# The down product of a SwiGLU block as seven block products (Strassen) in place of eight, interleaved with the next slab's first gate and up units

## The reference

```python
SEQ, D_MODEL, D_FF = 512, 2048, 5632
def reference(x, norm_mix_g, norm_ffn_g, nsa_w_in, ..., ffn_w_gate, ffn_w_up, ffn_w_down):
    h = rms_norm(x, norm_mix_g[i])
    x = x + nsa_mixer(h, ...)
    h = rms_norm(x, norm_ffn_g[i])
    x = x + (silu(h @ wg) * (h @ wu)) @ wd
```

## Time and profile before

| | us |
|---|---|
| median of 3 runs | 2411.09 (2411.08 to 2411.6) |
| profiled execution, first to last instruction (span) | 2406.7 |
| the median less that span | 4.4 |
| last piece of unbroken PE work in the chain that ended last | 967.95 to 2399.60 |
| end of the last add into x2 | 2402.11 |

### The profile page before, as it was taken

The page is one execution under the profiler, slowest core; times in us unless marked ns, Lnnn a source line. Parts: engine busy times, 40 slices in busy tenths (PEclk is TensorE's granted clock), DMA queues, the critical chain, the costliest instruction groups (busy, mean ns, idle before and its releaser), DMA issues.

```text
span 2406.7 us, 32223 instructions
## 1 busy us (share of the span) xinstructions
PE 2359.4 (98%) x12347; PEld 2021.5 (84%) x12347; DVE 1082.1 (45%) x1852; ACT 698.1 (29%) x1081; POOL 38.6 (2%) x44
## 2 busy tenths in 40 slices
PE   7999999999999999999999999999999999999998
PEld 6898888888889899888888888888888888888887
DVE  5333566665665556433334334343433333333433
ACT  4332344443452334322212122222222221212221
POOL 1000000000010000000000000000000000000000
PEclk9999999999999999999999999999999999999999
DMA  5333211212113212332333333333333233332333
GB/s 174 114 110 90 69 54 46 71 53 63 53 62 132 71 62 80 95 98 89 105 96 96 96 94 98 96 96 96 96 97 96 94 101 99 95 97 89 102 96 114
DMA packets 212815, 218.62 MB, mean 91 GB/s; under 512 B 12715, under 2 KB 186816, under 8 KB 211440
## 3 DMA queue, kind: packets, MB, share of 16 engines
q1 hardware_dynamic: 211792, 211.86, 28.3%
q0 software_dynamic: 928, 5.44, 0.7%
HBM read 213.05 MB, written 4.19 MB: 90 GB/s over the span
## 4 chain that ended last, share of the span: by engine, by line
PE 95%; DVE 3%; ACT 1%; issue 1%; DMA 0%; POOL 0%; DVEq 0%; SPq 0%; ACTq 0%
PE ps L1057 93%; PE ps L1351 1%; DVE wl L623 0%; DMA x_rows<-in_x_dram 0%; PE ps L1343 0%; DVE x_rows L639 0%; DVE nmax L888 0%; PE ps L1387 0%; DVE ptl L908 0%; ACT ptc L369 0%; DVE pbuf L902 0%; ACT sq L372 0%; DVE x_rows L824 0%; DVE ql L623 0%; DVE hTl L623 0%
## 5 line engine op out<-in xcount | busy, mean ns | idle before, releaser
L623 DVE TENSOR_TENSOR wl<-raw,wh 128x1024 fp32r<-128x1024 f32 x386 | 472.3, 1224 | 754.4 <-ACT wh L369 753.4
L1057 PE MATMUL ps<-hTh,wh 128*128 128x512 f32 (+1 forms) x1968 | 768.5, 391 | 6.7 <-DVE wl L623 3.5
L1057 PE MATMUL ps<-hTh,wl 128*128 128x512 f32 (+1 forms) x1968 | 761.9, 387 | 0.0
L1057 PE MATMUL ps<-hTl,wh 128*128 128x512 f32 (+1 forms) x1968 | 761.1, 387 | 0.0
L369 ACT ACTIVATE wh<-raw 128x1024 fp32r<-128x1024 f32 x386 | 408.7, 1059 | 1016.8 <-PE ps L1057 998.0
L1057 PEld LDWEIGHTS ps<-hTh,wh 128*128 128x128 f32 x1968 | 371.5, 189 | 78.9 <-DVE ql L623 3.6
L1057 PEld LDWEIGHTS ps<-hTh,wl 128*128 128x128 f32 x1968 | 370.7, 188 | 75.1
L1057 PEld LDWEIGHTS ps<-hTl,wh 128*128 128x128 f32 x1968 | 371.1, 189 | 71.6
L1057 PE MATMUL ps<-wh,mTl 128*128 128x512 f32 x704 | 274.3, 390 | 0.0
L1057 PE MATMUL ps<-wh,mTh 128*128 128x512 f32 x704 | 274.3, 390 | 0.0
L1057 PE MATMUL ps<-wl,mTh 128*128 128x512 f32 x704 | 274.3, 390 | 0.0
(11 more groups left out here) (164 smaller groups left out, 1655.0 us busy)
## 6 DMA issues: line engine op xcount, KB each, us to landing
raw<-in_ffn_w_gate_dram SPq DMA_DIRECT2D x176, 256.0 KB, 2.9
raw<-in_ffn_w_up_dram SPq DMA_DIRECT2D x176, 256.0 KB, 2.9
raw<-in_ffn_w_down_dram SPq DMA_DIRECT2D x176, 256.0 KB, 3.2
raw<-in_nsa_w_in_dram SPq DMA_DIRECT2D x164, 256.0 KB, 3.0
raw<-in_nsa_w_out_dram SPq DMA_DIRECT2D x64, 256.0 KB, 3.0
x_rows<-in_x_dram SPq DMA_DIRECT2D x4, 1024.0 KB, 12.2
raw<-in_nsa_cmp_w_dram SPq DMA_DIRECT2D x16, 256.0 KB, 3.0
x_rows<-in_x_dram POOLq DMA_DIRECT2D x4, 1024.0 KB, 7.6
```

The costliest lines, as they stand in the source:

```text
L623: nc.vector.tensor_tensor(dst, src, hi.bitcast(f32), ALU.subtract).then_inc(done, 1)
L1057: return nc.tensor.matmul(out_, a, b, start=start, stop=stop, skip_group_check=True)
```

## The change

The down product of one slab is Y[512 tokens x 2048] += m[512 x 512] W[512 x 2048]. It is now done as two quads of 1024 output columns. In a quad each operand is taken as 2 x 2 blocks, and Strassen's method in Winograd's form needs seven block products where eight stood. A block product (`product`) is 12 matmuls of 128x512 on a weight block of 128x1024 (256 rows of W by 512 columns); it fills two banks. So a slab has 14 down units of 12 matmuls (d0 to d13), and its 16 gate and up units (g0 to g15) stay as they were.

The combinations of weight blocks are made by DVE in `down` and `t3` (`add`: four per quad), and split like any unit. The combinations of m are made by DVE at up units 7 and 15 (four subtractions or adds of 128x256), after which ACT rounds seven operands to `opsh` (three copies) and DVE subtracts to `opsl` (three `lo`). `operands_at` says where that is done: for the second half at g15, for the first half, in a mixed slab, only at d13, since `opsh` and `opsl` of the slab before are in use until then. DVE adds two banks at a time to `x2` after each block product (`down_out`), and PE waits for the add of d(j-2) before d(j).

The down units of a slab no longer follow its own g15. They are mixed with the next slab's first gate and up units: g0 g1 d0 d1, six times (g, d, d), then g8 to g15. The last slab's 14 down units stand alone at the end (`DOWNS`). Slab 0 has only g units (`UPS`); the loop runs over pairs of slabs. The down blocks are loaded into four buffers of their own. At the end there are eight stores of 512 KB.

Core of the diff (ACT's `up_split` and `down_split`, the memory and semaphore declarations and the calls of `slab` on ACT and DVE are left out):

```diff
+G_UNITS, QUAD, DOWN = 16, 7, 14
+TURN = G_UNITS + DOWN
+UPS = [("g", j) for j in range(G_UNITS)]
+MIXED = [("g", 0), ("g", 1), ("d", 0), ("d", 1)] \
+    + [e for r in range(6) for e in (("g", 2 + r), ("d", 2 + 2 * r), ("d", 3 + 2 * r))] + UPS[8:]
+DOWNS = [("d", j) for j in range(DOWN)]
+LEFT = [M0A, M1A, S2, S1, S3, N4, M1B]
...
+        def down_bank(j):
+            return 4 + 2 * ((j // QUAD + j % QUAD) % 2)
+        def operands_at(order, j):
+            if order is DOWNS or order is UPS or j == G_UNITS - 1:
+                return ("g", j)
+            return ("d", DOWN - 1)
...
@@ SP
+                    quad, o = j // QUAD, j % QUAD
+                    if o in (2, 3, 5, 6) and (s < SLABS or quad == 0):
+                        wait(sp, lo_ready, n0 + p + 1, 2 * TURN, i)
+                        down_block({2: 0, 3: 1, 5: 3, 6: 2}[o], s - 1 + quad, i, 1 - quad)
...
@@ ACT
-                    if j in (7, 15):
-                        for c in range(2):
-                            wait(act, m_ready, (j - 7) // 4 + c + 1, 4, s)
-                            copy(mTh[:, (j - 7) // 4 + c, :], ffn_work[:, 2 + c, :]).then_inc(m_hi, 1)
+                    for b in range(2):
+                        if (kind, j) == operands_at(order, 8 * b + 7):
+                            wait(act, m_ready, 2 * s + b + 1, 4, i)
+                            wait(act, units_used, n0 + p + 1, 2 * TURN, i)
+                            copy(opsh[:, b, M0A, :], ffn_work[:, 2, 0:256]).then_inc(m_hi, 1)
+                            copy(opsh[:, b, M1A:M1B + 1, :]..., ffn_work[:, 3, :]).then_inc(m_hi, 1)
+                            wait(act, m_sums, 2 * s + b + 1, 4, i)
+                            copy(opsh[:, b, S1:N4 + 1, :]..., ffn_work[:, 0:2, :]...).then_inc(m_hi, 1)
...
@@ DVE
+            def down_out(n, s, i, j):
...
+                wait(dve, units_used, n + 1, 2 * TURN, i)
+                if after:
+                    wait(dve, y_added, before + after, 2 * DOWN, i)
+                nc.vector.tensor_tensor(at, at, ps[:, down_bank(j):down_bank(j) + 2, :], op).then_inc(y_added, 1)
...
+                        own.done(nc.vector.tensor_tensor(s1, m0b, m1b, ALU.subtract))
+                        nc.vector.tensor_tensor(s3, m0a, m0b, ALU.subtract)
+                        own.settle()
+                        own.done(nc.vector.tensor_tensor(s2, s1, m0a, ALU.subtract))
+                        own.settle()
+                        nc.vector.tensor_tensor(n4, m1a, s2, ALU.add).then_inc(m_sums, 1)
+                    for b in range(2):
+                        if (kind, j) == operands_at(order, 8 * b + 7):
+                            wait(dve, m_hi, 6 * s + 3 * b + 1, 12, i)
+                            lo(opsl[:, b, M0A, :], ffn_work[:, 2, 0:256], opsh[:, b, M0A, :], m_lo)
...
+                    if kind == "d":
+                        down_out(n, s, i, j)
+                    if p + RING < len(ahead):
+                        turn, (what, unit) = ahead[p + RING]
+                        (up_split if what == "g" else down_split)(n + RING, turn, i, unit)
...
@@ PE
+            def product(n, j):
+                o, b = LEFT[j % QUAD], down_bank(j)
+                for tt in range(2):
+                    for kk in range(2):
+                        ts, at = slice(tt * P, (tt + 1) * P), slice(kk * 512, (kk + 1) * 512)
+                        last = mm3(bank(b + tt), (opsh[:, kk, o, ts], opsl[:, kk, o, ts]),
+                                   (wh[:, n % RING, at], wl[:, n % RING, at]), kk == 0 and j % QUAD in (0, 1, 3), kk == 1)
+                last.then_inc(units_used, 1)
...
+                    wait(pe, lo_ready, n + 1, 2 * TURN, i)
+                    if kind == "d":
+                        if j == 0:
+                            wait(pe, m_lo, 6 * s, 12, i)
+                        if j >= 2:
+                            wait(pe, y_added, DOWN * (s - 1) + j - 1, 2 * DOWN, i)
+                        product(n, j)
+                        continue
...
+                    if s and j == 8:
+                        wait(pe, y_added, DOWN * s, 2 * DOWN, i)
+                    hidden_unit(n, j)
```

More of the change, by code:

```diff
@@ L301, in _, with up_unit @@
-            out_v = out[0].rearrange("(t p) d -> p t d", p=P)
[L302 to L306, removed]
+            def up_unit(n, s, i, j):
+                b, q, w = j // 8, j % 8 // 2, (w_gate_v, w_up_v)[j % 2]
+                src = w[q][:, :, bass.ds(i * 1024 + s * 512 + b * 256, 256)]
+                for dst, half in k_halves(n, src, 4):
+                    sp.dma_start(dst, half).then_inc(raw_loaded[n % RAW], 16)
@@ new lines, in _ @@
+            out_v = out[0].rearrange("(t p) d -> p t d", p=P)
+            for quad in range(2):
+                for done, row, half in ((2, 0, 0), (5, 2, 1), (6, 0, 1), (7, 2, 0)):
+                    at = (slice(None), slice(row, row + 2), slice(quad * 1024 + half * 512, quad * 1024 + half * 512 + 512))
+                    sp.wait_ge(y_added, (SLABS - 1) * DOWN + quad * QUAD + done)
+                    sp.dma_start(out_v[at], x2[at]).then_inc(stored, 16)
+            sp.wait_ge(stored, 128)
@@ new lines, in slab @@
+            def slab(order, after, n0, s, i):
+                ahead = [(s, e) for e in order] + [(s + 1, e) for e in after]
+                for p, (kind, j) in enumerate(order):
+                    if s == 0 and j == 1:
+                        hidden_part(3)
+                    if kind == "g" and j in (6, 14):
+                        wait(act, gs_ready, 2 * s + j // 8 + 1, 4, i)
+                        nc.scalar.activation(ffn_work[:, 0:2, :], ffn_work[:, 0:2, :], ACT.Silu).then_inc(silu_done, 1)
+                    for b in range(2):
[3 more added lines that the diff above has]
+                            copy(opsh[:, b, M0A, :], ffn_work[:, 2, 0:256]).then_inc(m_hi, 1)
+                            copy(opsh[:, b, M1A:M1B + 1, :].rearrange("p o c -> p (o c)"), ffn_work[:, 3, :]).then_inc(m_hi, 1)
+                            wait(act, m_sums, 2 * s + b + 1, 4, i)
+                            copy(opsh[:, b, S1:N4 + 1, :].rearrange("p o c -> p (o c)"),
+                                 ffn_work[:, 0:2, :].rearrange("p a c -> p (a c)")).then_inc(m_hi, 1)
+                    if p + RING < len(ahead):
+                        turn, (what, unit) = ahead[p + RING]
+                        (up_split if what == "g" else down_split)(n0 + p + RING, turn, i, unit)
@@ L617, in _ @@
+            slab(UPS, MIXED[:RING], F0, 0, 0)
+            with act.Fori(0, PAIRS) as i:
+                for h in range(2):
+                    slab(MIXED, MIXED[:RING], F0 + G_UNITS + h * TURN, 1 + h, i)
+            slab(MIXED, MIXED[:RING], F0 + G_UNITS + (SLABS - 3) * TURN, SLABS - 2, 0)
+            slab(MIXED, DOWNS[:RING], F0 + G_UNITS + (SLABS - 2) * TURN, SLABS - 1, 0)
+            slab(DOWNS, [], F0 + G_UNITS + (SLABS - 1) * TURN, SLABS, 0)
         @block.vector
@@ L1008, in _, with up_split, add @@
             last.then_inc(r2_diag, 1)
[L1010 to L1013, removed]
+            def up_split(n, s, i, j):
+                wait(dve, hi_ready, n + 1, 2 * TURN, i)
+                lo(wl[:, n % RING, :], raw[:, (F0 + s * G_UNITS + j) % RAW, :], wh[:, n % RING, :], lo_ready)
+            def add(out_, a, b):
+                nc.vector.tensor_tensor(out_, a, b, ALU.add).then_inc(sums_ready, 1)
@@ L1014, in slab @@
+            def slab(order, after, n0, s, i):
+                ahead = [(s, e) for e in order] + [(s + 1, e) for e in after]
+                both = rbc[:, :].rearrange("p (a c) -> p a c", a=1).to_broadcast([P, 2, S])
+                for p, (kind, j) in enumerate(order):
+                    n, b = n0 + p, j // 8
+                    if s == 0 and j == 1:
                         hidden_part(3)
-                    if first and j == 4:
+                    if s == 0 and j == 4:
                         dve.wait_ge(rb_done, 1)
@@ L1037, in slab @@
[L1037 to L1046, removed]
@@ new lines, in slab @@
+                    if kind == "d":
+                        down_out(n, s, i, j)
+                    if p + RING < len(ahead):
+                        turn, (what, unit) = ahead[p + RING]
+                        (up_split if what == "g" else down_split)(n + RING, turn, i, unit)
+            slab(UPS, MIXED[:RING], F0, 0, 0)
+            with dve.Fori(0, PAIRS) as i:
+                own.enter(i, 12)
+                for h in range(2):
+                    slab(MIXED, MIXED[:RING], F0 + G_UNITS + h * TURN, 1 + h, i)
+                own.leave(PAIRS)
@@ L1417, in norm_bcast, with hidden_unit @@
                 last.then_inc(rb_done, 1)
-            def hidden_unit(n, j, per, s):
+            def hidden_unit(n, j):
                 for half in range(2):
                     columns_half(n, j % 8 // 2, half, j // 8 * 4 + j % 2 * 2 + half)
[L1424 to L1428, removed]
+            def product(n, j):
```

(20 more changed lines are left out.)

166 lines of the change are left out of this document (100 added, 66 removed).

## The result

| | before | after |
|---|---|---|
| median, us | 2411.09 (4 runs) | 2439.61 (4 runs, 2437.68 to 2443.74) |
| ratio to before, 95% interval | | 1.0119 [1.0105, 1.0133] |
| span of the profiled execution, us | 2406.7 | 2436.6 |

The change makes the kernel 28.5 us slower. The forecast was 2431, so it is 8.6 us too low; the measured time lies inside the forecast's own range of 2417 to 2446, in its upper quarter.

The account below looks back on a forecast made before the run. PE, busy 98% of the span, was taken as the bound. Terms: -59.8 + 56 + 9.2 - 1.3 - 1.0 + 16.5 = +19.6 us on the 2406.7 span, plus 4.4 to the median: 2431 us; own range 2417 to 2446.

Parts of the forecast that it names:

- The 59.8 us: Down matmuls on PE fall from 192 to 168 a slab, 264 fewer at 0.2267 us each: -59.8 us.
- the third rival: DVE's chain around d13 is shorter than counted: 2360 us if hidden altogether, 2394 with half the wait left; chance 0.06.
- The wait at g8: In each mixed slab PE's g8 waits for DVE's add of d13: 5.6 us, ten times, +56 us.
- The walk: DVE's operations from g7's end on PE to the add of d13 at 10.8 us; g8 starts 5.4 us late.
- The rounds: Mix rounds (g, d, d): DVE needs 11.0 us against PE's 10.88, covered by the ring, costed at nothing.
- The fourth rival: The mix rounds stall too, through DVE's work and late loads: 2 us more a slab, 2451 us; chance 0.08.
- The clock: PE's granted clock falls to half after ten g8 waits and the tail's: 11 x 1.5 = +16.5 us.
- the first rival: The waits are there but the clock stays up: 2414 us, or 2408 to 2422; chance 0.13.
- The second rival: Long cold stretches of 10.2 us follow the waits: 2465 us; chance 0.08.
- The tail: Last slab's down units: d0 waits 6.65 us for m_lo, d7 about 0.6, d8 about 1.9; +9.2 us.
- The end and the start: At the very end, the last store is 512 KB in place of 1024 KB: -1.0 us.

Follow-up runs that it names:

- e5: e4 with DVE's add of d13 also put ahead of the sums of m and the opsl subtractions: 2360.59 us, ratio 0.9794 to the kernel before.
- e1: Kernel after, with DVE's add of d13 issued before the three opsl subtractions: 2418.32 us, ratio 1.003 to the kernel before.
- e2: Kernel after, with g8 waiting only for the add of d12 and g9 for that of d13: 2376.75 us, ratio 0.9859 to the kernel before.
- e4: e2 with the four 128x256 sums of m of the first half made at d13 instead of g7: 2367.41 us, ratio 0.982.
- e3: Kernel after, with 24 matmuls of 128x512, result never read, run on PE ahead of g8's wait: 2419.22 us, ratio 1.0034.
- e6: e5 with d0, d1 and d2 each waiting only for the part of m_lo that they use: 2360.30 us, ratio 0.9784.

## Why the prediction was right, and where it was off

**What bounds.** PE did, and its cadence stayed 0.2267 us with `opsh` as stationary operand: in e5 it shows 3089 matmuls in 700 us, the same spacing. The 59.8 us were there to be had; e5 has them less the tail, and the 2360 us of the third rival, priced for this case, were met at 2360.59.

**The wait at g8.** Mechanism, place and size were right: 5.59 us for 5.6. The last tenths are luck: the walked steps give 5.4, and 5.6 was chosen between that and 6.2. The walk was right step by step: sums done at 4.23 us (measured 1132.44 - 1128.08 = 4.36), add of d12 6.50 (6.64), add of d13 10.8 (10.97). e1 and e2 took pieces out of the chain and the wait fell to 3.4 and 1.1 us, and in e4 to nothing at g8 and 0.3 us at g9. The names in the wait list (L1134 and once `opsl`) and the count of ten at g8 were as forecast.

**The rounds.** Costed at nothing, and they cost nothing: no wait of PE is left between 1000 and 2280 us in e5, with all of DVE's work still in it. The fourth rival is out. Its 11.0 us against 10.88 were also too high: DVE's operations of 1024 columns start 1.13 to 1.14 us apart when nothing holds them, so nine of them take 10.2 us.

**The clock.** The mechanism was right: two of two early waits pointed to it, the first rival (clock stays up) is out, e3 shows 20 us. Its size was too small, and this is the largest error in the sum: 1.5 us a wait taken, 2.2 measured. Two things were missing. The cold stretch was taken as 3.4 us from the earlier trace rows; in the first slab PE works 3.5 us of it, in the nine later ones 4.0 to 4.9 us, by the spacing of the matmuls. And the first matmul after a long wait takes 0.59 us to the next one's start, 0.16 more than the cadence of 0.43 at half clock. At both early waits the clock fell 0.3 and 0.7 us after PE was back and stayed low for 3.4 us. Here it falls while PE stands and stays low for 6.8 us, of which the part after the restart is paid in matmuls; the later the fall, the larger that part. Why a dip lasts 3.4 us in one case and 6.8 in another is open. The second rival's 10.2 us did not appear. One reading of the sum was loose too: of the counts of 8 and 7 in the earlier trace rows, the 8 are from windows that are in part at full clock; the share of 0.45 does come out of the starts in the trace, though, 0.21 us apart against 0.12.

**The tail.** d0's wait was 6.61 (6.65 forecast). The two later ones are 1.83 each, where 0.6 and 1.9 were walked. The missed piece is a transfer: ACT's split for d8 waits 2.81 us in all, the last part for the reload of a down block, which the chain of waits puts at 3.85 us from 2401.21 on. I had costed the loads at nothing for the whole stage; in the tail, without g units between, that cover is gone. DVE's split for d8 waits 1.08 us for ACT there, which is about what the two waits are above the walked sum (3.66 for 2.5). No run moved that load, so its share is read from the chain and not shown by an edit. ACT's row, and the piece of the chain:

```profile
2405.08 1.06 ACT L427 ACTIVATE wh<-down 128x1024 fp32r<-128x1024 f32 x1 [2.81 <-DMA down<-in_ffn_w_down_dram]
```

```profile
2401.21 3.85 DMA down<-in_ffn_w_down_dram
```

**The end and the start.** -1.4 for -1.0. The 1.6 us ahead of the block were no step of the prediction and are not caused by the change.

## What to carry to other kernels

Fewer matmuls pay only as long as the engine that feeds TensorE finishes each hand-over in time: walk that engine's queue instruction by instruction between two neighbouring units, above all where a once-per-slab job stands ahead of the one result that TensorE waits for. Let a wait name the buffer that is overwritten and not "all adds so far": here that one number and two moved blocks of code turned +28 into -50 us. Price a wait of TensorE with its clock, here from about 2 us on, and look for that in windows of a microsecond, since the page's slices hide it. Where executions differ ahead of the part that was changed, compare that part alone, from one event in the trace to another.

## What the runs showed of the hardware

- A wait of 1.09 us among dense matmuls left the granted clock at full in ten of ten cases (e2). In the tail, waits of 1.61 to 1.76 us left it at full (the kernel after, e3, e4, e5); behind waits of 1.95 (e6), 1.97 (e1) and 2.48 us (e2) it fell to half, each time 1.4 us after PE was back. Waits of 3.4 and 5.4 us brought slowdowns of 2.0 and 2.2 us a slab on average, and the granted clock at 0.98 over the stage.
- Costs that I had expected to shrink with the wait do not: cutting it from 5.4 to 3.4 us left the clock's share nearly whole (2.2 and 2.0 us). A dip lasts 6.8 us after all ten waits of 5.4 us, and 3.4 (seven times) or 6.8 us (three times) after those of 3.4 us, but after the longer wait 1.9 to 3.4 us of it pass while PE still stands.
- On DVE, 128x1024 operations in a row start 1.13 to 1.14 us apart while each shows 1.22 us; a chain of them is to be counted with the smaller number, except behind a wait.
- Two banks of PSUM read by one DVE instruction take 1.216 us (154 of them), where two of one bank each took 2 x 0.682.
